# First conv tap moved to ScalarE, softplus and the activation sums cut into pieces between the sums of block products

## What is computed

```
def project(h):
    zxbcdt = h @ in_w
    z = zxbcdt[..., :D_INNER]
    xbc = silu(centred_dwconv(zxbcdt[..., D_INNER:D_INNER + CONV_DIM], conv_w, conv_b))
    dt_raw = zxbcdt[..., D_INNER + CONV_DIM:]
    xs, bm, cm = xbc[..., :D_INNER], xbc[..., D_INNER:D_INNER + GN], xbc[..., D_INNER + GN:]
    dt_f = softplus(dt_raw[..., :SSM_HEADS] + dt_bias[0])
    dt_b = softplus(dt_raw[..., SSM_HEADS:] + dt_bias[1])
...
cum = cumsum(dt * a)                      # within chunks of 128 tokens
y = (scan forward) + flip(scan backward) + xs * d_skip
out = rmsnorm(y * silu(z), norm_w) @ out_w
```

## Time and profile before

| | us |
|---|---|
| median of 3 runs | 1460.6 (1460.18 to 1460.69) |
| the profiled execution | 1461.46 |
| its span, first to last instruction | 1459.7 |
| PE busy | 1343.7 |
| DVE busy | 680.5 |
| ACT busy | 409.2 |
| POOL busy | 275.3 |
| mean granted clock of PE | 0.973 |

### The profile page before, as it was taken

The page is one execution under the profiler, slowest core; times in us unless marked ns, Lnnn a source line. Parts: engine busy times, 40 slices in busy tenths (PEclk is TensorE's granted clock), DMA queues, the critical chain, the costliest instruction groups (busy, mean ns, idle before and its releaser), DMA issues.

```text
span 1459.7 us, 30536 instructions
## 1 busy us (share of the span) xinstructions
PE 1343.7 (92%) x12917; PEld 917.8 (63%) x12917; DVE 680.5 (47%) x1154; ACT 409.2 (28%) x1032; POOL 275.3 (19%) x258
## 2 busy tenths in 40 slices
PE   5988989998999799999999999999999989999876
PEld 2466766676667688755566556688757855565432
DVE  4585988767776865651222222152363532221112
ACT  2312244454545310221222222222152302221111
POOL 0322352535265600000111111000000001111100
PEclk9999999999999999999999999999999989999988
DMA  9754344334531641525999999876321289999993
GB/s 346 283 173 144 116 143 147 129 132 145 202 117 37 181 129 60 208 110 184 396 397 389 383 378 381 349 253 219 108 106 53 81 305 363 392 395 398 401 406 144
DMA packets 132222, 338.78 MB, mean 232 GB/s; under 512 B 13363, under 2 KB 63339, under 8 KB 125803
## 3 DMA queue, kind: packets, MB, share of 16 engines
q1 hardware_dynamic: 122571, 313.38, 58.8%
q0 software_dynamic: 6208, 12.60, 2.5%
q10 hardware_dynamic: 3296, 10.73, 2.0%
HBM read 327.88 MB, written 16.91 MB: 236 GB/s over the span
## 4 chain that ended last, share of the span: by engine, by line
PE 64%; DMA 8%; DVE 7%; SPq 4%; issue 4%; ACT 2%; POOL 1%; DVEq 0%; ACTq 0%; POOLq 0%
PE ps L1852 14%; PE ps L1475 9%; PE ps L1891 7%; PE ps L1722 6%; PE ps L1782 4%; SPq L673 3%; DMA tmp<-in_moe_w_up 2%; PE ps L2181 2%; PE ps L1913 2%; PE ps L2091 2%; PE ps L1395 2%; DMA ssb<-in_moe_w_down 1%; PE ps L1551 1%; SPq L675 1%; DMA tmp<-in_shared_w_down 1%
## 5 line engine op out<-in xcount | busy, mean ns | idle before, releaser
L1852 PE MATMUL ps<-ring,ssb 128*32 128x256 f32 x2368 | 138.3, 386 | 6.5 <-DMA ring<-in_moe_w_up 6.5
L2786 DVE COPY big<-ps 32x256 f32<-32x256 f32 x162 | 68.6, 423 | 145.7 <-PE ps L1891 144.0
L2777 DVE TENSOR_TENSOR ssb<-ssb,ps 128x128 f32<-128x128 f32 (+1 forms) x56 | 19.5, 348 | 247.9 <-ACT ssb L1199 247.9
L1852 PEld LDWEIGHTS ps<-ring,ssb 128*32 128x32 f32 x2368 | 80.7, 112 | 58.9 <-DMA ring<-in_moe_w_up 9.9
L1475 PE MATMUL ps<-hT,own 128*128 128x256 f32 x456 | 109.6, 389 | 2.7 <-POOL own L861 2.6
L1475 PEld LDWEIGHTS ps<-hT,own 128*128 128x128 f32 x456 | 85.2, 193 | 25.1 <-issue 14.1
L1212 ACT COPY big<-ps 32x256 f32<-32x256 f32 x162 | 58.6, 362 | 141.1 <-PE ps L1891 139.6
L1852 PE MATMUL ps<-tmp,ssb 128*32 128x256 f32 x1568 | 88.7, 379 | 4.8 <-DMA tmp<-in_moe_w_up 4.7
L1199 ACT ACTIVATE ssb<-ps 128x128 f32<-128x128 f32 (+1 forms) x56 | 18.2, 324 | 249.3 <-PE ps L1852 249.3
L936 POOL DMA_INDIRECT y_rows<-big,sidx x32 | 30.0, 938 | 304.9 <-DVE big L2786 304.1
L2367 DVE SCALAR_TENSOR_TENSOR ring<-ring,par 128x512 f32<-128x512 f32 x96 | 85.6, 892 | 3.4
(11 more groups left out here) (463 smaller groups left out, 2429.0 us busy)
## 6 DMA issues: line engine op xcount, KB each, us to landing
ring<-in_ada_w SPq DMA_DIRECT2D x44, 1024.0 KB, 5.0
ring<-in_moe_w_gate SPq DMA_DIRECT2D x60, 512.0 KB, 12.4
ring<-in_moe_w_up SPq DMA_DIRECT2D x60, 512.0 KB, 16.0
ring<-in_moe_w_down SPq DMA_DIRECT2D x28, 1024.0 KB, 17.3
ring<-in_ssd_in_w SPq DMA_DIRECT2D x20, 1024.0 KB
tmp<-in_moe_w_down SPq DMA_DIRECT2D x20, 1024.0 KB, 17.5
tmp<-in_moe_w_gate SPq DMA_DIRECT2D x37, 512.0 KB, 12.5
tmp<-in_moe_w_up SPq DMA_DIRECT2D x37, 512.0 KB, 16.1
```

Of the source, the lines that this page charges most:

```text
L1852: ins = pe.matmul(tiled_gu[32 * c:32 * c + 32, 2 * h + i, :].rearrange("p (r n) -> p r n", r=2), XgT[l][:, k * C + 32 * g:k * C + 32 * g + ...
L2786: ins = dve.tensor_copy(Y[s % 2][32 * g:32 * g + 32, 256 * c:256 * c + 256], tiled_y[32 * c:32 * c + 32, 2 * h + i, :])
```

## The change

The first tap of each conv, with its bias, is taken from DVE and made on ACT (`conv_first_tap`, an Identity activation with scale and bias by partition). In a window both taps stand behind `take(w, 0)`; `conv_tanh(2w-2)` moves behind `take(w, 2)`. In the steps the taps of the last chunks stand at `FIRST_TAP_AT`. Both taps and both tanh count on one semaphore. `softplus` is cut into ten parts, placed in windows 1 to 4 ahead of the sums, and the bank copy `ada_rows(1)` now opens window 4. What hangs on softplus moves by a window: ln of dt, the cumulative sums, `decays`, `cum_copies` (its two spreads become `spread_cum`, around the last two sums of window 5) and `split_cum` (in halves, windows 6 and 7). The copy `dtT` goes ahead of `t1` to `t4`. `activation_sums` is cut in halves of two instructions; the slices move back by one place. GpSimd's and SP's lists are the same.

```diff
+FIRST_TAP_AT = {1: (2, 18), 5: (0, 20), 8: (2, 22)}
...
+            def conv_first_tap(i):
...
+                elif i % 2:
+                    act.wait_ge(s_ds, sum_made(pair, 4))
+                    act.wait_ge(s_pre, product_taken(pair, 6))
+                else:
+                    act.wait_ge(s_ds, sum_made(pair, 5))
+                if i >= 2:
+                    act.wait_ge(s_sil, i - 1)
+                act.activation(cacc[i % 2].rearrange("p (s n) -> p s n", s=2), pre[i % 2][:, :, 0:S], ACT.Identity,
+                               bias=par[:, 272 + ch:273 + ch], scale=par[:, ch:ch + 1]).then_inc(s_th, 1)
...
                 take(w, 0)
+                conv_first_tap(2 * w - 2)
+                conv_first_tap(2 * w - 1)
                 if w == 8:
                     act.wait_ge(s_ln, 2)
                     decay_exps(0, 0)
-                conv_tanh(2 * w - 2)
-                if w == 8:
                     decay_exps(0, 1)
                 take(w, 2)
+                conv_tanh(2 * w - 2)
...
             def conv(i):
...
-                link(dve.tensor_scalar(o, pre[i % 2][:, :, 0:S], par[:, ch:ch + 1], par[:, 272 + ch:273 + ch],
-                                       ALU.mult, ALU.add))
+                dve.wait_ge(s_th, first_tap_made(i))
...
             for w in range(1, FIRST_STEP_PAIR):
+                if w == 4:
+                    ada_rows(1)
                 conv(2 * w - 2)
-                if w in (2, 3):
-                    softplus({2: 1, 3: 3}[w])
-                elif w == 4:
+                if w in (2, 3, 4):
+                    softplus({2: 2, 3: 5, 4: 8}[w])
+                elif w == 5:
                     cum_copies()
...
+                    modulation(1)
+                elif w == 7:
+                    split_cum(0, 1)
                 sum_product(w, 1)
...
-                if w in (1, 2):
-                    softplus({1: 0, 2: 2}[w])
-                elif w == 4:
-                    ada_rows(1)
+                if w in (1, 2, 3, 4):
+                    softplus({1: 0, 2: 3, 3: 6, 4: 9}[w])
                 elif w == 5:
-                    split_cum(0)
+                    spread_cum(0)
+                elif w == 7:
+                    split_cum(1, 0)
                 sum_product(w, 4)
...
+                if w in (1, 2, 3):
+                    softplus({1: 1, 2: 4, 3: 7}[w])
+                elif w == 5:
+                    spread_cum(1)
+                elif w == 6:
+                    split_cum(0, 0)
+                elif w == 7:
+                    split_cum(1, 1)
                 sum_product(w, 5)
...
             for j, i in enumerate(TAIL_PAIRS):
                 gate(10 + 2 * j)
+                if j:
+                    activation_sums(0, 0)
                 sum_product(i, 1)
                 gate(11 + 2 * j)
-                activation_sums(j)
+                if j:
+                    activation_sums(0, 1)
                 sum_product(i, 4)
                 sum_product(i, 5)
+            activation_sums(1, 0)
             for n in range(3):
                 weight_sum(0, n)
+            activation_sums(1, 1)
             gate(14)
             gate(15)
```

More of the change, by code:

```diff
@@ L205, in sum_made, with first_tap_made, tanh_made @@
     return 3 * (s - 1) + SUM_COUNT[r]
+def first_tap_made(c):
+    return 4 * (c // 2) + c % 2 + 1
+def tanh_made(c):
+    return 4 * (c // 2) + c % 2 + 3
 def pair_bank(s, r):
@@ L1597, in _ @@
                     turn_b(0)
-                elif w == 5:
-                    pe.wait_ge(s_cumv, 5)
-                    for d in range(2):
-                        for t in range(NT):
-                            ins = pe.transpose(ps[:, 6 + d, t * P:(t + 1) * P], ncum4[:, d, t * P:(t + 1) * P], ident)
-                    ins.then_inc(s_cT, 1)
                 elif w == 8:
@@ L1637, in _ @@
                     pe.matmul(ps[:, 5, 256:512], ones[:, :], sp[6], start=True, stop=True).then_inc(s_cT, 1)
+                elif w == 5:
+                    pe.wait_ge(s_cumv, 5)
+                    for d in range(2):
+                        for t in range(NT):
+                            ins = pe.transpose(ps[:, 6 + d, t * P:(t + 1) * P], ncum4[:, d, t * P:(t + 1) * P], ident)
+                    ins.then_inc(s_cT, 1)
                 elif w in (6, 7):
@@ L2316, in cum_copies, with spread_cum, split_cum @@
                 dve.tensor_tensor(wdt[:, :, :], cdec[:, :, :], ncum[:, :, :], ALU.add).then_inc(s_cumv, 1)
-                for d in range(2):
-                    dve.tensor_copy(ncum4[:, d, :].rearrange("p (t j h) -> p t j h", t=NT, j=4),
-                                    ncum[:, :, d * NH:(d + 1) * NH].unsqueeze(2).to_broadcast([P, NT, 4, NH])).then_inc(s_cumv, 1)
-            def split_cum(d):
-                dve.wait_ge(s_cT, 2)
+            def spread_cum(d):
+                dve.tensor_copy(ncum4[:, d, :].rearrange("p (t j h) -> p t j h", t=NT, j=4),
+                                ncum[:, :, d * NH:(d + 1) * NH].unsqueeze(2).to_broadcast([P, NT, 4, NH])).then_inc(s_cumv, 1)
+            def split_cum(d, part):
                 mid = sz[0][:, 0:T // 2].bitcast(BF16)
                 rest = yb[d]
-                link(dve.tensor_copy(cparts[:, d, :], ps[:, 6 + d, :]))
-                link(dve.tensor_tensor(rest, ps[:, 6 + d, :], cparts[:, d, :], ALU.subtract))
+                if part == 0:
+                    dve.wait_ge(s_cT, 2)
+                    link(dve.tensor_copy(cparts[:, d, :], ps[:, 6 + d, :]))
+                    link(dve.tensor_tensor(rest, ps[:, 6 + d, :], cparts[:, d, :], ALU.subtract))
+                    return
                 link(dve.tensor_copy(mid, rest))
@@ L2544, in _ @@
                 gate(10 + 2 * j)
+                if j:
+                    activation_sums(0, 0)
                 sum_product(i, 1)
                 gate(11 + 2 * j)
-                activation_sums(j)
+                if j:
+                    activation_sums(0, 1)
                 sum_product(i, 4)
                 sum_product(i, 5)
+            activation_sums(1, 0)
             for n in range(3):
                 weight_sum(0, n)
+            activation_sums(1, 1)
             gate(14)
             gate(15)
-            activation_sums(2)
+            for part in range(2):
+                activation_sums(2, part)
             weight_sum(0, 3)
-            activation_sums(3)
+            for part in range(2):
+                activation_sums(3, part)
             def term(p, r):
```

70 lines of the change are left out of this document (37 added, 33 removed).

## The result

| | before | after |
|---|---|---|
| median of 4 runs each, us | 1460.6 | 1474.7 (1472.7 to 1476.5) |
| ratio, with its 95% interval | | 1.0093 (1.0074 to 1.0111) |
| the profiled execution, us | 1461.46 | 1472.66 |
| its span, us | 1459.7 | 1470.9 |
| mean granted clock of PE | 0.973 | 0.974 |

What follows compares the result with a forecast made beforehand. TensorE, busy 92% of the span, was taken as the bound, so other engines count only where it waits. Windows +8.9, steps -2.0 and tail -1.4 gave +5.5 us on the 1460.6 median: 1466.1 us, range 1456 to 1473.

Steps and rivals of the forecast that it cites:

- What goes: Pair windows: PE's two 5.4 us waits at 95.29 and 126.24, their clock drops and a 0.8 us wait vanish, 17.5 us.
- First stretch: Windows 2 to 8, mainly before product 3: DVE's sum comes late behind ACT's tap and the pieces, 10.6 us of new waits.
- Second stretch: Windows 2 to 7, before product 6 or its like: DVE late beside GpSimd's weight sums, 9.7 us, bounds 3 and 12.4.
- Third stretch: Last sum of a window, needed by the next product 0: waits in windows 1 (1.0) and 7 (2.5), 3.5 us.
- The clock: Pair windows: the short new waits bring one half-clock drop like the first, 2.6 us, between 0 and 9.
- rival D: Windows: short waits cluster and three drops come, 9 us for 2.6, +11.9, 1472.5 us; chance 0.15.
- Windows in sum: Net of the pair windows, new waits and clock less the waits that go: +8.9 us.
- Steps: 200 to 475 us: eight chunks lose a TENSOR_SCALAR on DVE, shortening PE's waits, -2.0 us, between 0 and -3.5.
- Tail: Activation sums moved by a pair, in halves: one wait and drop go, waits at pair 19 and gate 14 grow, -1.4 us.
- the -5.8: Tail: PE's 4.14 us wait at 489.20 and the 1.7 lost to the drop behind it both go.
- B: Windows before product 6: GpSimd meets little, that stretch costs 3, not 9.7; -1.2, 1459.4 us; chance 0.20.
- C: Windows: DVE catches up, its taps run undisturbed beside GpSimd and no clock drop comes; -9.3, 1451.3 us; chance 0.15.

Runs made afterwards that it cites:

- taps_early: Changed kernel with both first taps of a window ahead of ScalarE's take of product 0 instead of behind it: 0.9963 of the kernel before, 1453.2 against 1458.2 us.
- short_weight_sums: Changed kernel with GpSimd's weight sums for pairs 2 to 8 cut to a quarter of their columns (only its time counts): 0.9917, 1447.0 against 1459.9 us before.
- pad_two: Changed kernel with two extra matmuls (0.86 us) on PE ahead of product 1 of pair 1, results overwritten: 1.0100 of the kernel before.
- step_taps_on_dve: Kernel with taps ahead of the take and softplus, split_cum and gates re-placed, but first taps of chunks 16 to 23 back on DVE: 0.9888 of the kernel before.
- tail_as_before: Changed kernel with activation sums as before (slice 0 whole in pair 18, slice 1 in pair 19): 1.0089 of the kernel before, the same as the change.

## Why the prediction was wrong, step by step

**What goes: right.** By starts the two waits were 5.58 and 5.48 us, their drops cost 3.06 and 2.79, the small wait 0.92: 17.8, forecast 17.5.

**First stretch: right.** 10.1 against 10.6. The chain is as worked out. Of ScalarE, window 2 (take, then both taps), and all taps by shape (count, busy us, mean ns):

```profile
77.51 0.37 ACT L1026 COPY tmp<-ps 128x256 f32<-128x256 f32 x1 [1.15 <-PE ps L1511]
77.91 1.52 ACT L1044 ACTIVATE ring<-ring,par 128x512 f32<-128x512 f32 x2
```

```profile
L1044 ACT ACTIVATE ring<-ring,par 128x512 f32<-128x512 f32 x24 | 18.2, 808 | 0.0
```

The tap takes 0.808 us, estimated at 0.80. DVE's conv starts at 78.76, 3.25 us after product 0 at 75.51; 2.14 + 0.27 + 0.80 = 3.21 was the estimate. taps_early and short_weight_sums show from both sides that this term hangs on the taps' place: it all but goes with the first (1.4 us stay) and stays, to 0.02 us, with the second.

**Second stretch: right in size, by two errors that cancel.** 9.0 against 9.7: window 2 had nothing of its 2.1, and the other four windows 1.4 more than forecast. short_weight_sums shows GpSimd to be its cause. Of DVE in window 2 after the change, two of softplus' instructions beside GpSimd's first two sums (87.99 and 89.48), for 0.42 and 0.29 alone:

```profile
88.31 1.37 DVE L2334 TENSOR_TENSOR ssb<-ssb 128x256 f32<-128x256 f32 x1
89.72 1.25 DVE L2335 TENSOR_SCALAR ssb<-ssb 128x256 f32<-128x256 f32 x1
```

The Trainium skill (SBUF — State Buffer, "Who interferes with whom") gives the exclusion by whole instructions; the rows agree, and show it for a TENSOR_SCALAR with one tensor input too. Window 2 itself has no such wait, because of the drop at 84.7; in pad_two, without that drop, the wait is there. The drop did two things. It slowed PE by 1.7 us, and it put off GpSimd, whose sums wait for PE: the first starts 3.62 us after product 3 in the change and 2.14 in pad_two. So DVE's four taps ran clear of it. DVE and GpSimd in the change, then in pad_two:

```profile
84.24 3.11 DVE L2399 SCALAR_TENSOR_TENSOR ring<-ring,par 128x512 f32<-128x512 f32 x4
...
87.99 1.41 POOL L870 TENSOR_TENSOR own<-ring 128x512 f32<-128x512 f32 x1 [13.24 <-PE ps L1511]
```

```profile
84.81 4.09 DVE L2402 SCALAR_TENSOR_TENSOR ring<-ring,par 128x512 f32<-128x512 f32 x4
...
87.09 1.27 POOL L870 TENSOR_TENSOR own<-ring 128x512 f32<-128x512 f32 x1 [11.77 <-PE ps L1514]
```

The silu behind them took 0.69 against 1.76 us. **Third stretch: too small.** 5.2 against 3.5: I had counted waits in windows 1 and 7 and left out 0.7 and 0.6 in windows 2 and 6, which have two instructions ahead of the last sum as well. In window 2 these two take 1.82 us beside GpSimd; in window 6 it is the silu ahead of them that does (1.42 us), and they add their 1.4.

**The clock: this step failed, by the size of its term.** "I count one drop like the first: 2.6 us, between 0 and 9." Four came in the windows, 7.0 us. My ground was that the drops seen came behind waits of 4 and 5 us, and one of 2.04 late in the stage. But the kernel before had a drop at 207.12 us too, behind waits of 1.31, 1.39 and 1.00 us close together; the stretch from 190 to 220 us stood at 0.94 in my view of the clock, and I passed over it:

```profile
207.12:210.53 3.41, 3.41 (x23) 3.08 (x24) 3.27 (x6) 0.00 (x0) 0.00 (x0) 0.50 1.09 414
```

With thirteen waits of 1 to 3 us, several drops were the likely case. That was rival D in kind. That its total, 1472.5, comes so near is partly luck: it priced three drops at 3 us each where four of 1.7 came in the windows, and had none in the steps.

**Windows in sum:** 24.3 + 7.0 - 17.8 = 13.5 us; from the first product of pair 1 to the second set of cum rows in window 8 the span grew from 128.27 to 141.23 us, 13.0. Forecast 8.9. The other 0.5 us may come from how the starts are counted and from waits too short for a bracket; the runs don't settle it.

**Steps: the waits right, the rest not.** PE's waits in the steps add up to 23.7 us before and 21.2 after, -2.5 (forecast -2.0); the one behind `take_cb` fell from 2.4 to 1.0. In one step "On ACT two taps more lie beside its idle time" was wrong: the taps go ahead of the exps that DVE and then PE need.

```profile
373.90 1.52 ACT L1044 ACTIVATE ring<-ring,par 128x512 f32<-128x512 f32 x2
```

```profile
378.00 1.09 PE L1600 MATMUL ps<-ssb 128*64 128x128 f32 x16 [0.84 <-issue]
```

That wait is new; the one behind it shrank from 0.68 to 0.27, so it cost 0.4 us, inside the 2.5; in step_taps_on_dve, without the taps on ACT, it is gone. What turned the sign was the second step that failed: two more stretches at half clock than before, 3.4 us, behind waits that are no new ones. The first row is PE of the kernel before, the second that wait after the change:

```profile
282.73 0.41 PE L1521 MATMUL ps<-cparts,c 128*64 128x128 bf16 x8 [2.16 <-DVE tmp L2403]
```

```profile
292.06 0.41 PE L1557 MATMUL ps<-cparts,c 128*64 128x128 bf16 x8 [2.16 <-DVE tmp L2435]
```

The same 2.16 us; before, the clock stayed at 1.00 behind it (282.7 to 289 us), after it fell to 0.5 for 3.41 us. I had no term for this. Steps in sum +0.8 instead of -2.0 (the lag goes from 13.0 to 13.7 us at pair 18).

**Tail: right in size by luck of signs.** -1.0 against -1.4. The wait of 1.6 us ahead of product 6 of pair 19 did not come. But the -5.8 was relative: in tail_as_before the old tail's wait is 2.45 us, not 4.14. A half-clock stretch just ahead of it (from 492.84 us) has slowed PE by 1.7 there, and the wait is shorter by 1.7, so DVE has caught up by that. So the new tail wins nothing over the old one.

**Sum:** 13.0 + 0.8 - 1.0 = 12.8 us up to the end of the output projection (12.7 by the trace), against 5.5. The clock makes all of the gap of 7.2 us: 4.4 is the windows' clock term and 3.4 the drops in the steps, and the rest is -0.6. The medians are 14.1 apart (10.8 to 16.2 by the interval), the two profiled executions only 11.2, because the first product of pair 1 started 2.0 us earlier in the trace after; that start lies between 59.1 and 61.6 us in all traces, whatever the kernel. So the last one or two microseconds can't be placed.

**The rivals.** B and C rested on GpSimd meeting little; short_weight_sums is close to C made true, but for one drop: 12 us under before, where C was worked out at 9.3. The range ended at 1473 because D was given 0.15 and its price stopped at three drops in the windows, with none for the steps.

## What to carry to other kernels

A step moved to an idle engine still has a place in that engine's list: behind a copy that waits for the matmul engine it came 2 us late, and DVE sat idle for 37 us waiting for it; ahead of the copy that fell to 17 us, and the whole kernel was 18.5 us faster. Cut a long piece where the other user of the port is silent and where the engine waits anyway; pieces in the shadow of GpSimd's sums took two to four times as long, and moving them and two gates, with no work removed, was worth more (13 us, some 4 of them in the tail) than moving the tap (nothing to be told from the medians, at the end). And where the trace of before shows drops behind short waits, as at 207.12 us here, price each new wait of about 2 us or more on TensorE as the wait and a good part of a drop: 14 of 20 such waits in the windows of three traces had one, of 1.7 us or more.
